# Moving the weight buffers of a two-layer kernel to other addresses in SBUF

## The chip, the cores and the metric

The kernel runs on one core of a Trainium2 chip. The metric is the device time of one execution in microseconds; three runs of the kernel before gave 1261.37, 1260.05 and 1260.09 us, median 1260.09 us. One of these executions was taken with the profiler.

## The reference

The reference computes two layers of a transformer on a sequence of 512 tokens, model width 1024, all in float32. Layer 0 has sparse attention (16 heads of 64, an indexer that keeps the best 128 keys of each query, a T5 bias); layer 1 has latent attention (16 heads, queries and keys of 96, values of 64). Each is followed by a feed-forward block with a causal convolution of width 3. Cut to what matters here:

```
for layer in range(2):
    h = rms_norm(x, norm_mix[layer])
    m = mixer_a(h, ...) if layer == 0 else mixer_b(h, ...)   # both end in  out @ w_out
    x = x + m
    h = rms_norm(x, norm_ffn[layer])
    u = h @ f_w_up[layer]                                    # 1024 -> 5632
    u = conv_b + sum(conv_w[j] * shifted(u, j) for j in range(3))
    gate, val = split(u, 2)
    x = x + (silu(gate) * val) @ f_w_down[layer]             # 2816 -> 1024
```

The feed-forward width is 2816, that is 22 tiles of 128.

## The kernel before

Every large product is done in three matmuls, so that the result is close to float32: each operand x is split into a rounded part x_hi and the rest x_lo, and `product3` (its three matmuls are lines 1715, 1716 and 1717) adds hi*hi, then s_hi*m_lo, then s_lo*m_hi into the same bank of PSUM. The first operand after the destination is the stationary one (loaded into the array, PEld in the profile), the second is streamed past it.

Weights come in units of up to 1 MB (128 partitions of 2048 words). The unit with number u goes to slot u % 2 of three buffers, each `[128, 2, SLOT]` words with SLOT = 2048:

- SyncE starts the DMA into `raw[:, s]` (`load`, line 389) once the unit two before it has been split;
- ScalarE copies it, rounded, to `w_hi[:, s]` (`hi`, line 571);
- VectorE writes `w_lo = raw - w_hi` (`lo`, line 937). Ten units of the first stage are split by GpSimd instead (line 527).

TensorE waits for `w_lo_done` before it uses a slot. Everything is ordered by semaphores written by hand; each engine has its own list of instructions, in program order.

The stages, in order of time: input products of mixer A (to about 190 us; here the tokens `h_hi`, `h_lo` are stationary and the weights are streamed in stretches of 512 columns); attention A (to about 270); its output product; feed-forward 0, up (325 to 566; weights stationary, `h_hi`, `h_lo` streamed) and down (567 to 675; weights stationary, `a_hi`, `a_lo` streamed); the latent stages of mixer B (688 to 775; its first product streams the weights in stretches of 416 columns), attention B, its output product, and feed-forward 1. At the joins between stages VectorE adds the result to `xT` (line 1139) and prepares `h_lo` (line 943) for each of eight tiles, while ScalarE prepares `h_hi` (line 579) and GpSimd sums squares held in `v` (line 501).

All tensors in SBUF are laid one behind another in the order in which the code declares them, each starting at the next multiple of 32 bytes; a nested `with ExitStack() as scope` gives its space back at its end, so that what is declared behind it lies over it (`act` over `ckv_hi` and others; `probs` and `toep` over `h_hi` and `h_lo`; `a_hi` and what follows over `qT`). Tensors named `pad_...` are never written or read. In the built program `xT` starts 16,512 bytes into each partition. Counted from there, the places of the operands modulo 512 bytes are 0 for `raw`, `w_hi`, `w_lo`, `act`, `h_hi`, `h_lo`, `probs`, `toep_a1`, `toep_b0`, `toep_b1`, `a_hi` and `a_lo`, and 64 for `v`, `rope_tmp` and `cv`. Modulo 2048 bytes, `raw`, `w_hi`, `w_lo` and `act` are at 0, `h_hi`, `h_lo`, `probs`, `a_hi` and `a_lo` at 512, `v` at 64.

Of the kernel before, what the change touches and what calls it, by code (L numbers as in the profile page):

```python
# [21 lines left out]
F32 = mybir.dt.float32  # L22
F32R = mybir.dt.float32r
BF16 = mybir.dt.bfloat16
ALU = mybir.AluOpType
# [3 lines left out]
P = 128  # L29
S = 512  # L30
# [26 lines left out]
B_DOWN = Q_LORA + KV_LORA + ROT  # L57
# [5 lines left out]
CT = 2 * FT  # L63
UP_STEPS = FT // 2
SLOT = 2048

BLOCK_N = [128 * (b + 1) for b in range(T)]
ROW = sum(BLOCK_N)
# [24 lines left out]
U_UP = [U_AOUT + KD, 0]  # L93
# [22 lines left out]
def unit_words(u):  # L116
# [5 lines left out]
    if u < U_DOWN[0]:  # L122
        return SLOT
    if u < U_B:
# [3 lines left out]
    if u < U_UP[1]:  # L128
        return D
    return SLOT if u < U_DOWN[1] else D  # L130

# [32 lines left out]
def hybrid_layers_kernel(nc, xt, vectors, t5_bias, a_in_wide, a_in_small, a_w_out, b_w_down, b_w_uq,  # L164
# [4 lines left out]
    with ExitStack() as ctx:  # L169
        def sb(name, shape, dt=F32, scope=ctx):  # L170
            return scope.enter_context(nc.sbuf_tensor(name, shape, dt))

        def sem(name):
            return ctx.enter_context(nc.semaphore(name))


        xT = sb("xT", [P, KD, S])
        raw = sb("raw", [P, 2, SLOT])
        w_hi = sb("w_hi", [P, 2, SLOT], F32R)
        w_lo = sb("w_lo", [P, 2, SLOT], F32R)  # L180

        with ExitStack() as scope:
            sb("pad_act", [P, 5, S], F32, scope)
# [36 lines left out]
        sq = v[:].rearrange("p t (a n) -> p (t a) n", n=S)  # L220

        rope_tmp = sb("rope_tmp", [P, 2, H * HALF])
        sb("pad_level", [P, 112])


        with ExitStack() as scope:
# [17 lines left out]

        with ExitStack() as scope:
            qT = sb("qT", [P, 16, S], F32, scope)
        a_hi = sb("a_hi", [P, 2, S], F32R)
        a_lo = sb("a_lo", [P, 2, S], F32R)
        u_in = sb("u_in", [P, 4, S + 4])
        cv = sb("cv", [P, 4, S])  # L250
        rbc = sb("rbc", [P, S])
        diag = sb("diag", [P, T, P])
        sb("pad_q", [P, 16 * S - (4 * S + 4 * (S + 4) + 4 * S + 2 * S)])
        ps = ctx.enter_context(nc.psum_tensor("ps", [P, 8, 512], F32))


# [24 lines left out]
        w_raw = [sem("w_raw0"), sem("w_raw1")]  # L281
# [100 lines left out]
        @block.sync  # L382
        def _(sp):
            def load(u, src, dst=None, k=None):

                s = u % 2 if k is None else k
                if not isinstance(u, int) or u >= 2:
                    sp.wait_ge(w_lo_done, u - 1)
                sp.dma_start(dst if dst is not None else raw[:, s, :], src).then_inc(w_raw[s], 16)

            sp.dma_start(gain, vectors[:, 0:G_COLS]).then_inc(v_in, 16)
            sp.dma_start(xT[:, 0:2, :], xt[:, 0:2, :]).then_inc(x_in[0], 16)
            for s in range(2):
                load(U_A + s, a_in_small[s], raw[:, s, 0:4 * A_SMALL])
            sp.dma_start(bucket, bucket_of).then_inc(b_in, 16)
            sp.dma_start(t5, t5_bias).then_inc(b_in, 16)
            for j in range(1, 4):
                sp.dma_start(xT[:, 2 * j:2 * j + 2, :], xt[:, 2 * j:2 * j + 2, :]).then_inc(x_in[j], 16)
            sp.wait_ge(w_lo_done, U_A + 1)
            sp.dma_start(raw[:, 0, 0:D], a_in_wide[0, 0, :, 0:D]).then_inc(w_first, 16)  # L400
            sp.dma_start(raw[:, 0, D:SLOT], a_in_wide[0, 0, :, D:SLOT]).then_inc(w_raw[0], 16)
            sp.dma_start(vec[:, G_COLS:V_COLS], vectors[:, G_COLS:V_COLS]).then_inc(c_in, 16)
            sp.dma_start(con[:], constants).then_inc(c_in, 16)
            load(U_A + 3, a_in_wide[0, 1])
            for c in range(2, len(A_CHUNKS)):
                for s in range(2):
                    load(U_A + 2 * c + s, a_in_wide[c - 1, s])
                if c == 2:

                    sp.wait_ge(rows_sb, 2)  # L410
                    sp.dma_start(bias_rows, bias_sb).then_inc(bias_out, 16)
                if c == 3:
                    sp.wait_ge(bias_out, 16)
                    sp.dma_start(bias_tiles, bass.AP(bias_rows.tensor, P - 1, [[640, H], [-1, P], [1, S]]))\
                      .then_inc(bias_out, 16)
            for k in range(2):
                load(U_AOUT + k, a_out_v[k], raw[:, k, 0:D])

            def load_toep(i, e):
                sp.dma_start(toep[i % 2][e][:, :], bias_tiles[2 * i + e]).then_inc(toep_in[i % 2][e], 16)  # L420

            sp.wait_ge(bias_out, 32)
            sp.wait_ge(pa_half, len(A_CHUNKS))
            load_toep(0, 0)
            load_toep(0, 1)
            load_toep(1, 0)
            sp.wait_ge(pa_done, 4 * (len(A_CHUNKS) - 1))
            load_toep(1, 1)
            for i in range(2, PAIRS):
                for e in range(2):  # L430

                    sp.wait_ge(l_ok[0], 6 * (i - 2) + 5 + e)
                    load_toep(i, e)
            for k in range(2, KD):
                load(U_AOUT + k, a_out_v[k], raw[:, k % 2, 0:D])

            def load_ffn(l):
                with sp.Fori(0, UP_STEPS) as i:
                    for s in range(2):
                        load(U_UP[l] + 2 * i + s, f_up[l, i, s], raw[:, s, :], s)  # L440
                with sp.Fori(0, FT // 2) as i:
                    for s in range(2):
                        load(U_DOWN[l] + 2 * i + s, down_v[l][2 * i + s], raw[:, s, 0:D], s)

            load_ffn(0)

            load(U_B, b_w_down[0].rearrange("p (a n) -> p a n", a=2),
                 raw[:, 0, :].rearrange("p (a n) -> p a n", a=2)[:, :, 0:2 * B_DOWN])
            load(U_B + 1, b_w_down[1], raw[:, 1, 0:4 * B_DOWN])
            for s in range(2):  # L450
                load(U_B + 2 + s, b_uq_v[s], raw[:, s, 0:QW])
            for s in range(2):
                load(U_B + 4 + s, b_w_ukv[0, :, s * D:(s + 1) * D], raw[:, s, 0:D])
            for k in range(KD):
                load(U_BOUT + k, b_out_v[k], raw[:, k % 2, 0:D])
            load_ffn(1)

            for k in range(KD):
                sp.wait_ge(x_new[4], k + 1)
                sp.dma_start(out[:, k, :], xT[:, k, :]).then_inc(out_sem, 16)  # L460
            sp.wait_ge(out_sem, 16 * KD)
# [3 lines left out]
        def _(pool):  # L465
# [57 lines left out]
            for u in range(POOL_LO[0], POOL_LO[1]):  # L523
                pool.wait_ge(w_hi_done, u + 1)
                pool.wait_ge(w_lo_done, u)
                s = u % 2
                pool.tensor_tensor(w_lo[:, s, :], raw[:, s, :], w_hi[:, s, :].bitcast(F32), ALU.subtract)\
                    .then_inc(w_lo_done, 1)
            for u in range(UNITS):
                normed(0, u)  # L530
# [1253 lines left out]
```

## Time and profile before

| what | value |
|---|---|
| median of three runs | 1260.09 us |
| the profiled execution | 1261.37 us, of it 1259.6 us span |
| TensorE (PE) busy | 1220.7 us, 97% of the span |
| VectorE, ScalarE, GpSimd busy | 767.4, 547.5, 212.6 us |
| TensorE's granted clock, mean | 0.996 of 2.4 GHz |
| moved by DMA | 110.83 MB, 88 GB/s |

The span runs from the first to the last instruction of the profiled execution; what lies around it is 1261.37 - 1259.6 = 1.8 us. Matmuls overlap, and their ends are modelled: the time that one adds is the distance between the starts of two neighbours, not the duration shown for it. A group of the profile is a line of the code with the tile written and the tiles read; the order of the names in `h_hi,w_hi` does not tell which is stationary, the code does.

### The profile page before, as it was taken

The numbers are of one execution on the slowest core, as the hardware profiler recorded it, in microseconds if no ns is written. First come the engines' busy times: TensorE is split into PE (matmuls) and PEld (weight loads), VectorE is DVE, ScalarE is ACT, GpSimd is POOL, SyncE is SP. The second block draws the span as 40 slices with busy tenths as digits, with TensorE's granted clock in tenths as the row PEclk, the third lists the DMA queues.
The fourth block names the chain that finished last, engine by engine and source line by source line (L and its number), as shares of the span: only waits on it lengthen the run. The fifth ranks groups of instructions, "written<-read, shape, count | busy, mean of one in ns | idle before, by whom it ended". The sixth has DMA issues, their size and how long they took to land.

```text
span 1259.6 us, 17234 instructions
## 1 busy us (share of the span) xinstructions
PE 1220.7 (97%) x6072; PEld 980.3 (78%) x6080; DVE 767.4 (61%) x1337; ACT 547.5 (43%) x933; POOL 212.6 (17%) x262
## 2 busy tenths in 40 slices
PE   6999999999999999999999878999999999999998
PEld 4868886678788888888888766768788888887887
DVE  3577895754766666563337678762775666664334
ACT  5554435653633333332325676652543333343232
POOL 4314243430400000000003572430400000000000
PEclk9999999999999999999999999999999999999999
DMA  6432212204222232213332110012322222222323
GB/s 232 155 98 87 96 68 68 73 29 134 100 100 100 76 107 84 100 50 100 100 100 97 59 35 1 1 35 90 113 99 100 100 100 100 74 75 84 100 89 111
DMA packets 25120, 110.83 MB, mean 88 GB/s; under 512 B 2752, under 2 KB 3136, under 8 KB 17776
## 3 DMA queue, kind: packets, MB, share of 16 engines
q1 hardware_dynamic: 25072, 110.21, 25.8%
q8 instruction: 28, 0.46, 0.1%
q14 instruction: 20, 0.16, 0.0%
HBM read 108.06 MB, written 6.33 MB: 91 GB/s over the span
## 4 chain that ended last, share of the span: by engine, by line
PE 86%; DVE 6%; POOL 2%; ACT 2%; issue 2%; DMA 1%; SPq 0%; DVEq 0%; ACTq 0%; POOLq 0%
PE ps L1715 24%; PE ps L1717 24%; PE ps L1716 24%; PE ps L1476 3%; PE ps L1495 3%; PE ps L1376 2%; PE ps L1364 2%; DVE h_lo L943 1%; DVE xT L1139 1%; PE ps L1459 1%; DVE w_lo L937 1%; PE ps L1449 1%; PE ps L1359 1%; DMA xT<-in_xt 1%; POOL rope_tmp L479 1%
## 5 line engine op out<-in xcount | busy, mean ns | idle before, releaser
L937 DVE TENSOR_TENSOR w_lo<-raw,w_hi 128x1024 fp32r<-128x1024 f32 (+4 forms) x114 | 194.7, 1708 | 255.1 <-ACT w_hi L571 255.1
L1715 PE MATMUL ps<-h_hi,w_hi 128*128 128x512 f32 (+1 forms) x712 | 278.4, 391 | 2.4 <-DVE w_lo L937 2.4
L1716 PE MATMUL ps<-h_lo,w_hi 128*128 128x512 f32 (+1 forms) x712 | 277.7, 390 | 0.0
L571 ACT ACTIVATE w_hi<-raw 128x1024 fp32r<-128x1024 f32 (+4 forms) x124 | 177.7, 1433 | 229.8 <-PE ps L1717 229.5
L1717 PE MATMUL ps<-h_hi,w_lo 128*128 128x512 f32 (+1 forms) x712 | 277.5, 390 | 0.0
L1715 PE MATMUL ps<-a_hi,w_hi 128*128 128x512 f32 x480 | 188.0, 392 | 2.1 <-DVE w_lo L937 1.5
L1716 PE MATMUL ps<-a_lo,w_hi 128*128 128x512 f32 x480 | 186.8, 389 | 0.0
L1717 PE MATMUL ps<-a_hi,w_lo 128*128 128x512 f32 x480 | 186.8, 389 | 0.0
L1715 PEld LDWEIGHTS ps<-h_hi,w_hi 128*128 128x128 f32 (+1 forms) x712 | 133.5, 188 | 31.8 <-DVE w_lo L937 3.2
L1717 PEld LDWEIGHTS ps<-h_hi,w_lo 128*128 128x128 f32 (+1 forms) x712 | 133.6, 188 | 28.6 <-issue 0.6
L1716 PEld LDWEIGHTS ps<-h_lo,w_hi 128*128 128x128 f32 (+1 forms) x712 | 133.6, 188 | 28.1 <-issue 0.4
L786 ACT ACTIVATE cv<-u_in,vec 128x512 f32<-128x512 f32 x88 | 71.5, 816 | 187.4 <-DVE u_in L1165 185.4
L501 POOL TENSOR_TENSOR v<-v 128x512 f32<-128x512 f32 x28 | 50.7, 1810 | 462.5 <-ACT v L583 442.6
L1165 DVE TENSOR_TENSOR u_in<-ps,rbc 128x512 f32<-128x512 f32 x88 | 60.2, 688 | 94.3 <-PE ps L1717 91.5
L1715 PEld LDWEIGHTS ps<-a_hi,w_hi 128*128 128x128 f32 x480 | 90.1, 188 | 23.8 <-DVE w_lo L937 2.4
L1717 PEld LDWEIGHTS ps<-a_hi,w_lo 128*128 128x128 f32 x480 | 90.1, 188 | 18.8
L1716 PEld LDWEIGHTS ps<-a_lo,w_hi 128*128 128x128 f32 x480 | 90.1, 188 | 18.3
L1715 PE MATMUL ps<-w_hi,h_hi 128*128 128x512 f32 (+1 forms) x256 | 102.0, 398 | 2.4 <-DVE w_lo L937 1.9
L1717 PE MATMUL ps<-w_hi,h_lo 128*128 128x512 f32 (+1 forms) x256 | 99.5, 389 | 0.0
L1716 PE MATMUL ps<-w_lo,h_hi 128*128 128x512 f32 (+1 forms) x256 | 99.0, 387 | 0.0
L520 POOL TENSOR_SCALAR probs<-probs,inv_sum 128x256 f32<-128x256 f32 (+3 forms) x128 | 66.8, 538 | 106.7 <-DVE inv_sum L1024 106.5
L664 ACT ACTIVATE probs<-probs,neg_max 128x256 f32<-128x256 f32 (+3 forms) x128 | 70.5, 553 | 18.6 <-DVE neg_max L1014 18.4
(189 smaller groups left out, 1525.3 us busy)
## 6 DMA issues: line engine op xcount, KB each, us to landing
raw<-in_f_up SPq DMA_DIRECT2D x44, 1024.0 KB, 4.8
raw<-in_f_w_down SPq DMA_DIRECT2D x44, 512.0 KB, 3.4
raw<-in_a_in_wide SPq DMA_DIRECT2D x13, 1024.0 KB, 4.9
bias_tiles<-bias_rows SPq DMA_DIRECT2D x1, 4096.0 KB, 20.1
raw<-in_a_w_out SPq DMA_DIRECT2D x8, 512.0 KB, 3.4
raw<-in_b_w_out SPq DMA_DIRECT2D x8, 512.0 KB, 3.4
xT<-in_xt SPq DMA_DIRECT2D x4, 512.0 KB, 6.3
toep_b<-bias_tiles SPq DMA_DIRECT2D x8, 256.0 KB, 2.8
```

Of the source, the lines that this page charges most:

```text
L501: pool.tensor_tensor(total, total, sq[:, ORDER[n][k], :], ALU.add).then_inc(sq_sum, 1)
L520: ins = pool.tensor_scalar(x, x, inv_sum[:, slot, e, p:p + 1], 1.0, ALU.mult, ALU.mult)
L571: sc.activation(w_hi[:, s, 0:n], raw[:, s, 0:n], ACT.Copy).then_inc(w_hi_done, 1)
L664: ins = sc.activation(x, x, ACT.Exp, bias=neg_max[:, slot, e, p:p + 1], scale=-1.0, accum_out=sums[:, slot, e, p:p + 1])
L786: sc.activation(cv[:, q, :], u_in[:, q, 2:2 + S], ACT.Identity, bias=conv[:, 3, bass.ds(ch, 1)], scale=conv[:, 2, bass.ds(ch, 1)])\
L937: dve.tensor_tensor(w_lo[:, s, 0:n], raw[:, s, 0:n], w_hi[:, s, 0:n].bitcast(F32), ALU.subtract)\
L1165: dve.tensor_tensor(u_in[:, q, 2:2 + S], ps[:, 4 + q, :], rbc[:], ALU.mult).then_inc(f_in[l], 1)
L1476: ins = pe.transpose(ps[:, turn_bank(u, e), c * P:(c + 1) * P], probs[slot][:, e, c * P:(c + 1) * P], ident)
L1495: ins = pe.matmul(ps[e * DH:(e + 1) * DH, 7, b * P:(b + 1) * P], v[:, kb, h * DH:(h + 1) * DH], probsT[u % 2][:, e, c * P:(c + 1) * P], st ...
L1715: pe.matmul(dst, s_hi, m_hi, start=start, stop=False)
L1716: pe.matmul(dst, s_hi, m_lo, start=False, stop=False)
L1717: return pe.matmul(dst, s_lo, m_hi, start=False, stop=stop)
```

## The change

Each slot of `raw`, `w_hi` and `w_lo` becomes 16 words (64 bytes) longer, so slot 1 starts 64 bytes later within its buffer, and 96 words of padding follow each of the three buffers. `pad_level` (112 words ahead of `h_hi`) goes away, and `pad_a` (112 words ahead of `a_hi`, behind the place where `qT` begins) comes in; `pad_q` is shortened by the same 112 words. The remaining edits name the 2048 words that are used, `0:SLOT`, where the whole slot was named before.

```diff
+SLOT_PITCH = SLOT + 16
...
-        raw = sb("raw", [P, 2, SLOT])
-        w_hi = sb("w_hi", [P, 2, SLOT], F32R)
-        w_lo = sb("w_lo", [P, 2, SLOT], F32R)
+        raw = sb("raw", [P, 2, SLOT_PITCH])
+        sb("pad_raw", [P, 96])
+        w_hi = sb("w_hi", [P, 2, SLOT_PITCH], F32R)
+        sb("pad_w_hi", [P, 96])
+        w_lo = sb("w_lo", [P, 2, SLOT_PITCH], F32R)
+        sb("pad_w_lo", [P, 96])
...
         rope_tmp = sb("rope_tmp", [P, 2, H * HALF])
-        sb("pad_level", [P, 112])
...
             qT = sb("qT", [P, 16, S], F32, scope)
+        sb("pad_a", [P, 112])
         a_hi = sb("a_hi", [P, 2, S], F32R)
...
-        sb("pad_q", [P, 16 * S - (4 * S + 4 * (S + 4) + 4 * S + 2 * S)])
+        sb("pad_q", [P, 16 * S - (112 + 4 * S + 4 * (S + 4) + 4 * S + 2 * S)])
...
-                sp.dma_start(dst if dst is not None else raw[:, s, :], src).then_inc(w_raw[s], 16)
+                sp.dma_start(dst if dst is not None else raw[:, s, 0:SLOT], src).then_inc(w_raw[s], 16)
...
-                        load(U_UP[l] + 2 * i + s, f_up[l, i, s], raw[:, s, :], s)
+                        load(U_UP[l] + 2 * i + s, f_up[l, i, s], raw[:, s, 0:SLOT], s)
...
-                 raw[:, 0, :].rearrange("p (a n) -> p a n", a=2)[:, :, 0:2 * B_DOWN])
+                 raw[:, 0, 0:SLOT].rearrange("p (a n) -> p a n", a=2)[:, :, 0:2 * B_DOWN])
...
-                pool.tensor_tensor(w_lo[:, s, :], raw[:, s, :], w_hi[:, s, :].bitcast(F32), ALU.subtract)\
+                pool.tensor_tensor(w_lo[:, s, 0:SLOT], raw[:, s, 0:SLOT], w_hi[:, s, 0:SLOT].bitcast(F32), ALU.subtract)\
```

The places that result, in bytes from the start of `xT`, modulo 2048, with the shift of each:

| tensor | before | after | shift |
|---|---|---|---|
| raw, slot 0 / 1 | 0 / 0 | 0 / 64 | 0 / 64 |
| w_hi, slot 0 / 1 | 0 / 0 | 512 / 576 | 512 / 576 |
| w_lo, slot 0 / 1 | 0 / 0 | 1024 / 1088 | 1024 / 1088 |
| act | 0 | 1536 | 1536 |
| v, rope_tmp | 64 | 1600 | 1536 |
| h_hi, h_lo, probs, toep_a1, toep_b0, toep_b1, qT | 512 | 1600 | 1088 |
| a_hi, a_lo, u_in | 512 | 0 | 1536 |

On each of the five engines the program has the same instructions in the same order as before.

## Rows read from the trace of the kernel before

**Rows 1.** The page, busy time and share of the span of each engine.

```profile
PE 1220.7 (97%) x6072; PEld 980.3 (78%) x6080; DVE 767.4 (61%) x1337; ACT 547.5 (43%) x933; POOL 212.6 (17%) x262
```

**Rows 2.** The page, the chain that ended last, by engine.

```profile
PE 86%; DVE 6%; POOL 2%; ACT 2%; issue 2%; DMA 1%; SPq 0%; DVEq 0%; ACTq 0%; POOLq 0%
```

**Rows 3.** PE busy and its granted clock, in stretches of feed-forward and input products.

```profile
340.00:560.00 220.00, 220.00 (x973) 1.00 0.26 92
570.00:665.00 95.00, 95.00 (x421) 1.00 0.31 99
```

**Rows 4.** Groups by line and shape: xcount, busy us, mean ns, idle before.

```profile
L1715 PE MATMUL ps<-h_hi,w_hi 128*128 128x512 f32 x704 | 274.5, 390 | 2.4 <-DVE w_lo L937 2.4
L1715 PE MATMUL ps<-a_hi,w_hi 128*128 128x512 f32 x480 | 188.0, 392 | 2.1 <-DVE w_lo L937 1.5 <-DVE a_lo L1106 0.6
L1715 PE MATMUL ps<-w_hi,h_hi 128*128 128x512 f32 x224 | 89.9, 401 | 0.5 <-DVE w_lo L964 0.5
...
L937 DVE TENSOR_TENSOR w_lo<-raw,w_hi 128x2048 fp32r<-128x2048 f32 x45 | 105.4, 2342 | 58.0 <-ACT w_hi L571 58.0
L937 DVE TENSOR_TENSOR w_lo<-raw,w_hi 128x1024 fp32r<-128x1024 f32 x63 | 79.8, 1267 | 193.6 <-ACT w_hi L571 193.6
```

**Rows 5.** Timeline of PE in feed-forward 0, up: start, duration, operation.

```profile
450.26 0.39 PE L1715 MATMUL ps<-h_hi,w_hi 128*128 128x512 f32 x1
...
451.62 0.39 PE L1715 MATMUL ps<-h_hi,w_hi 128*128 128x512 f32 x1
```

**Rows 6.** The same in the input products of mixer A.

```profile
109.76 0.39 PE L1715 MATMUL ps<-w_hi,h_hi 128*128 128x512 f32 x1
...
112.48 0.39 PE L1715 MATMUL ps<-w_hi,h_hi 128*128 128x512 f32 x1
```

**Rows 7.** The same in the 416-column products of mixer B.

```profile
694.68 0.35 PE L1715 MATMUL ps<-w_hi,h_hi 128*128 128x416 f32 x1
...
695.24 0.35 PE L1715 MATMUL ps<-w_hi,h_hi 128*128 128x416 f32 x1
...
695.81 0.35 PE L1715 MATMUL ps<-w_hi,h_hi 128*128 128x416 f32 x1
...
696.37 0.35 PE L1715 MATMUL ps<-w_hi,h_hi 128*128 128x416 f32 x1
```

**Rows 8.** Line 1715, weight loads: ns min/median/max.

```profile
L1715 PEld LDWEIGHTS ps<-h_hi,w_hi x712: 140/188/238, 9.9 to 1134.6; 128*128 128x128 f32 x176, 128*72 128x72 f32 x2
L1715 PEld LDWEIGHTS ps<-a_hi,w_hi x480: 186/188/188, 270.3 to 1255.4; 128*128 128x128 f32 x160
```

**Rows 9.** DMA issues: size, median us to landing.

```profile
raw<-in_f_up SPq DMA_DIRECT2D x44, 1024.0 KB, 4.8
raw<-in_f_w_down SPq DMA_DIRECT2D x44, 512.0 KB, 3.4
...
toep_b<-bias_tiles SPq DMA_DIRECT2D x8, 256.0 KB, 2.8
...
rope_tmp<-bias_tiles SPq DMA_DIRECT2D x4, 256.0 KB, 2.7
toep_a<-bias_tiles SPq DMA_DIRECT2D x4, 256.0 KB, 2.9
```

**Rows 10.** Timeline, the splitting of one down unit, its load, its next use.

```profile
601.55 1.23 DVE L937 TENSOR_TENSOR w_lo<-raw,w_hi 128x1024 fp32r<-128x1024 f32 x1 [3.55 <-ACT w_hi L571]
...
602.95 0.33 SPq L389 DMA_DIRECT2D raw<-in_f_w_down  x1
...
611.34 1.06 ACT L571 ACTIVATE w_hi<-raw 128x1024 fp32r<-128x1024 f32 x1 [3.80 <-PE ps L1717]
```

**Rows 11.** Timeline of DVE and POOL at the join before feed-forward 0.

```profile
316.35 0.75 DVE L943 SCALAR_TENSOR_TENSOR h_lo<-xT,vec,h_hi 128x512 fp32r<-128x512 f32 x1
317.01 0.68 DVE L1139 TENSOR_TENSOR xT<-xT,ps 128x512 f32<-128x512 f32 x1
317.61 1.19 DVE L943 SCALAR_TENSOR_TENSOR h_lo<-xT,vec,h_hi 128x512 fp32r<-128x512 f32 x1
318.72 0.67 DVE L1139 TENSOR_TENSOR xT<-xT,ps 128x512 f32<-128x512 f32 x1
...
316.54 10.76 POOL L501 TENSOR_TENSOR v<-v 128x512 f32<-128x512 f32 x6 [46.22 <-ACT v L583]
```

**Rows 12.** The chain of waits at that join: start, us, what.

```profile
316.44 0.66 DVE h_lo L943
...
317.70 1.10 DVE h_lo L943
...
319.40 1.10 DVE h_lo L943
...
321.10 1.11 DVE h_lo L943
322.21 2.25 DVE w_lo L937
```

## Prediction

> **What bounds the kernel now.** I read the page first: TensorE is busy 1220.7 of 1259.6 us [rows 1], and the chain that ended last runs on it for 86%, on VectorE for 6%, GpSimd and ScalarE 2% each, DMA 1% [rows 2]. Then stretches within stages: in feed-forward up and down TensorE is busy all the time at a granted clock of 1.00, the 2.4 GHz level [rows 3]. The groups by shape give the size of it: 512-column matmuls come 3 x 704, 3 x 480 and 3 x 224 times (lines 1715, 1716 and 1717 alike), 4224 in all [rows 4]. What one adds is the distance of starts: six of them from 450.26 to 451.62 us make 0.2267 us each [rows 5], twelve from 109.76 to 112.48 also 0.2267 [rows 6]. So 4224 x 0.2267 = 957.6 us, 76% of the span, is a steady beat, and what the change does to that beat decides; the other engines matter at the joins between stages alone.
>
> **The change part by part.** It removes, adds and moves no instruction; each reads and writes as many words as before, and each DMA moves as many bytes in as many rows. Only places in SBUF differ. The question is therefore for each engine: does any row show that its time depends on the place?
>
> TensorE. In the two feed-forward blocks (3 x 704 up, 3 x 352 of the 3 x 480 down) and the output products (3 x 128) the weights are stationary: half of the loads then start at slot 1, 64 bytes past the 512-byte grid on which all of them lie now. The streamed `h_hi` and `h_lo` move to 64 past the grid as well, `a_hi` and `a_lo` stay on it. In the input products the roles are swapped. Three observations:
> - The beat is 0.2267 us with weights stationary and tokens streamed (places 0 and 512 modulo 2048) and also with the roles swapped [rows 5, 6]. There is no difference by which place does what.
> - The 416-column products of mixer B stream weights from starts 1664 bytes apart, so 0, 128, 256 and 384 bytes off the grid in turn. Each group of three takes 0.56 to 0.57 us (694.68, 695.24, 695.81, 696.37) whatever its start [rows 7]. That is 0.188 us a matmul, the duration of a weight load.
> - A weight load takes 188 ns in a beat of 226.7 [rows 8]. The 38.7 ns between are cover: a load from the new place could grow by a fifth and cost nothing.
> I take 0 for TensorE. No 512-column product has an operand at exactly 64 past the grid, so both bounds stay open. Above: the longest load of this kind of weights took 238 ns [rows 8]; if each from slot 1 did, (238 - 226.7) x 1776 = +20 us (1776 is half of the 3552 matmuls with stationary weights). Below: 512 columns at 2.4 GHz are 213.3 ns, so the beat has 13.3 ns that are not columns; if they were a conflict of places and went, 13.3 x 4224 = -56 us. I take the value of rows 5 to 7 as the nearest, since they vary the place and show nothing.
>
> The page "TensorE: Matmul & The Clock Gate" of the Trainium skill (section "Back-to-back issue gap") gives an isolated matmul N / 2.4 + 2.5 ns, that is 215.8 for 512 columns, and knows no term for where operands lie. The trace shows 226.7, so there are 10.9 ns which that formula does not explain; were they due to places, 4224 of them would be worth 46 us. By the formula itself the change gives nothing.
>
> VectorE, ScalarE, GpSimd on the weights. `w_lo` of 2048 words takes 2342 ns in the mean, of 1024 words 1267 [rows 4]: 1024 more words for 1075 ns, 1.05 ns a word, with both sources and the destination at the same place modulo 2048. A conflict that cost a second pass would show as twice that. I see no room for a gain, and take 0. They are hidden besides: in the feed-forward stretches TensorE never stopped for them [rows 3]. If each `w_lo` took a tenth less, the joins would gain about 0.2 us each, under 1 us in all.
>
> DMA. Every load for slot 1 now lands 64 bytes past the grid. The trace has this very case: `rope_tmp` lies 64 past it, `toep_a1` and the `toep_b` on it; the same 256 KB land in 2.7 us against 2.9 and 2.8 [rows 9]. So 0. The cover, should it be wrong: a down unit is free at 601.55 + 1.23 = 602.78, its load starts at 602.95, lands 3.4 later at 606.35, and ScalarE takes it at 611.34 after waiting for TensorE [rows 10]. The spare time is 5.0 us; a load would have to take 2.5 times as long before anything waited. The loads queue behind no other instruction of SyncE that has moved.
>
> The page "DMA: Bandwidth & Descriptors" of the Trainium skill ("How a descriptor splits into AXI transactions") speaks against the change: a row that does not start on a multiple of 256 bytes costs beats for the bytes before its start. The built program has `raw` at 32,896 bytes, which is 128 past such a multiple already; slot 1 goes to 192 past it. By the page that is 2 more beats of 32 bytes on some 260, an estimate of 0.04 us on 4.8, and it would be hidden. No row here can resolve that.
>
> GpSimd beside VectorE at the joins. While GpSimd sums squares (from 316.54), `h_lo` takes 1.19 us instead of 0.75, yet the addition to `xT` keeps its 0.67 to 0.68 [rows 11]. On the chain the four late pieces cost 1.10, 1.10, 1.11 and 2.25 us, where undisturbed ones are 0.66 and 1.23 (of a 1024-word `w_lo`, rows 10) [rows 12]. That is 0.44 x 3 + 1.02 = 2.3 us at this join; with three joins of this form, 7.0 us. It hits instructions with two sources in SBUF, at two quite different pairs of places (`xT`/`h_hi`, `raw`/`w_hi`), and spares the one whose other source is PSUM: so the ports are shared, not the places, and new places change nothing. The page "SBUF — State Buffer" of the Trainium skill ("Who interferes with whom") says the same, that a VectorE instruction with two SBUF inputs contends with a GpSimd instruction that reads SBUF. A rule of banks instead would let this go to zero.
>
> The sum: 0 + 0 + 0 + 0 on the profiled execution, 1259.6 of span and 1.8 around it, 1261.4 us. The median of the runs is 1.3 lower, so I forecast 1260.1.
>
> **The rivals.**
> A, slower: the loads of weights from slot 1 outgrow their cover. The place is the feed-forward and the output products, the price the +20 us above, so 1280 us. It decides from (2.5 / 1776 =) 1.4 ns a matmul on, that is from a load of about 228 ns, 40 more than now. For it: no weight load in the trace starts there, and single loads of 238 ns exist. Against: the cover, and rows 7. The same answer holds if the streamed `h_hi` costs a few cycles from its new start: at 2.4 ns for 2112 matmuls 5 us, 1265.
> B, faster: the slowdown beside GpSimd is a conflict of places, and the new spread ends it: 1260.1 - 7.0 = 1253 us. Against it speaks that two unlike pairs suffer alike [rows 11, 12].
> C, faster: part of the 13.3 ns in the beat is such a conflict, as weights and `h` share the 512-byte grid now. All of it gives 1204 us; 0.6 ns a matmul would be enough to see. Against: the beat does not care which roles the places have [rows 5, 6].
> D: the DMA into slot 1 is slower, but hidden: no change in time, only rows 9 would differ. It lies within my forecast.
> E: the change does not do what it says. The built program does have the new places, so there is nothing left of this one.
>
> **How the numbers follow.** No change 0.84 (of it 0.02 on either side for a small shift that is more than the bound), A with its small form 0.09, B 0.04, C 0.03. A measurement of this kernel tells about 0.2%, 2.5 us, from no change: the three runs are within 1.3 us. That makes faster 0.04 + 0.03 + 0.02 = 0.09, slower 0.09 + 0.02 = 0.11, and 0.80 for the same. The likeliest case alone ranges from 1257.6 to 1262.6. For 8 in 10 I give 1257.3 to 1263.0, a little wider upwards, where A's small form begins; the far ends of A (1280) and C (1204) and B are left out with less than 2 in 10.
>
> **What would show it.** Right: distances of starts of 0.2267 us in the same three stages; weight loads at 188 ns with both slots; `w_lo` at about 1227 and 2290 ns where undisturbed; loads of 4.8 and 3.4 us; the same four long pieces at the join. Wrong: for A, weight loads above 226 ns in every other unit, or a longer beat where `h_hi` streams; for B, 0.75 us for `h_lo` beside a busy GpSimd; for C, a beat below 0.226. The forecast fails as a whole if any place in SBUF sets TensorE's beat, by as little as 1 ns a matmul.

## The result: 0.6% slower, through TensorE's beat

The changed kernel took 1269.91 us (median of 7 runs, 1268.12 to 1272.72). The kernel before, run again beside it, took 1263.65 us (median of 7, 1260.05 to 1265.38). The ratio is 1.0057, with a 95% interval of 1.0039 to 1.0077. I had forecast 1260.1 us and no change; the time lies above the range of 1257.3 to 1263.0.

The page of the changed kernel, its shares by engine, and under them the chain that ended last:

```profile
span 1268.6 us, 17242 instructions
PE 1230.6 (97%) x6080; PEld 980.8 (77%) x6080; DVE 767.5 (60%) x1337; ACT 547.5 (43%) x933; POOL 212.5 (17%) x262
PE 87%; DVE 6%; POOL 2%; issue 2%; ACT 2%; DMA 1%; SPq 0%; DVEq 0%; ACTq 0%; POOLq 0%
```

Against [rows 1], PE is busy 9.9 us longer and the span is 9.0 us longer. VectorE, ScalarE, GpSimd and the weight loads are busy as long as before to within 0.5 us. So the added time is in the matmuls of TensorE. The groups by line and shape (count, busy us, mean ns of one, idle before; lines are four higher than before):

```profile
L1720 PE MATMUL ps<-h_lo,w_hi 128*128 128x512 f32 x704 | 275.6, 391 | 0.0
L1719 PE MATMUL ps<-h_hi,w_hi 128*128 128x512 f32 x704 | 275.4, 391 | 2.0 <-DVE w_lo L941 2.0
L1719 PE MATMUL ps<-a_hi,w_hi 128*128 128x512 f32 x480 | 189.5, 395 | 1.9 <-DVE w_lo L941 1.5 <-DVE a_lo L1110 0.4
L1719 PEld LDWEIGHTS ps<-a_hi,w_hi 128*128 128x128 f32 x480 | 90.2, 188 | 25.2 <-DVE w_lo L941 2.4 <-DVE a_lo L1110 1.3 <-issue 1.0
L941 DVE TENSOR_TENSOR w_lo<-raw,w_hi 128x2048 fp32r<-128x2048 f32 x45 | 105.4, 2341 | 58.0 <-ACT w_hi L575 58.0
L1719 PE MATMUL ps<-w_hi,h_hi 128*128 128x512 f32 x224 | 90.4, 404 | 0.0
L941 DVE TENSOR_TENSOR w_lo<-raw,w_hi 128x1024 fp32r<-128x1024 f32 x63 | 79.8, 1267 | 198.5 <-ACT w_hi L575 198.5
```

Against [rows 4] the means of the matmuls rise by 1 to 3 ns, while `w_lo` keeps 1267 ns and 2341 for 2342. The weight load keeps its 188 ns [rows 8]. The modelled durations hide the size of it; the starts give it. Feed-forward 0, up, in the changed kernel: first a stretch with the weights in slot 0, then one in slot 1 (start, duration):

```profile
345.41 0.39 PE L1719 MATMUL ps<-h_hi,w_hi 128*128 128x512 f32 x1
...
353.65 0.39 PE L1719 MATMUL ps<-h_hi,w_hi 128*128 128x512 f32 x1
...
357.08 0.39 PE L1719 MATMUL ps<-h_hi,w_hi 128*128 128x512 f32 x1
...
365.24 0.39 PE L1719 MATMUL ps<-h_hi,w_hi 128*128 128x512 f32 x1
```

Both pairs are 36 matmuls apart: 8.24 us, or 228.9 ns each, in slot 0, and 8.16 us, or 226.7 ns, in slot 1. Slot 0 is the slow one here, and it is slot 1 that the change moved off the grid. In down it is the other way round (slot 0, then slot 1):

```profile
576.15 0.39 PE L1719 MATMUL ps<-a_hi,w_hi 128*128 128x512 f32 x1
...
577.53 0.39 PE L1719 MATMUL ps<-a_hi,w_hi 128*128 128x512 f32 x1
...
580.93 0.39 PE L1719 MATMUL ps<-a_hi,w_hi 128*128 128x512 f32 x1
581.61 0.40 PE L1719 MATMUL ps<-a_hi,w_hi 128*128 128x512 f32 x1
...
584.41 0.40 PE L1719 MATMUL ps<-a_hi,w_hi 128*128 128x512 f32 x1
...
586.51 0.39 PE L1719 MATMUL ps<-a_hi,w_hi 128*128 128x512 f32 x1
```

In slot 1, 21 matmuls take 4.90 us, 233.3 ns each. In slot 0, which begins at 576.15, 15 take 3.40 us, 226.7 ns; its first six take 1.38 us, 230.0 ns each, so the slow beat of the slot 1 before runs on into them. What the two stages have in common is the distance between the two operands. In up, slot 0 holds weights on the grid while `h` is streamed from 64 bytes past it, and in slot 1 both are 64 past it. In down, `a` is on the grid and so is slot 0, while slot 1 is 64 past it.

The other engines and the DMA do not set this beat. The slot 1 stretch above, in two halves (busy time of PE, PEld, DVE, ACT, POOL, then granted clock, DMA share, GB/s):

```profile
581.60:584.40 2.80, 2.80 (x13) 2.26 (x12) 1.50 (x2) 1.58 (x2) 0.00 (x0) 1.00 0.07 28
584.40:587.20 2.80, 2.80 (x13) 2.26 (x12) 0.33 (x1) 0.00 (x0) 0.00 (x0) 1.00 0.61 186
```

VectorE and ScalarE work in the first half and hardly in the second, DMA the other way round, GpSimd in neither. The beat is 233.3 ns in both: 12 matmuls take 2.80 us up to 584.41, 9 take 2.10 us after it.

Where the 9.0 us went, as the distance from the start of the first to the start of the last 512-column matmul of each stage, both kernels by the profile:

(The first products with `w_out`, which run between pieces of attention, are left out of the output products.)

| stage | before, us | after, us |
|---|---|---|
| input products of mixer A | 185.77 | 187.40 |
| output products A, B | 38.61, 38.62 | 39.14, 39.18 |
| up 0, 1 | 243.17, 243.16 | 244.09, 244.09 |
| down 0, 1 | 120.58, 120.57 | 122.55, 122.55 |
| from down 0 to output product B | 171.56 | 172.18 |

That is 1.6 + 1.1 + 1.9 + 3.9 + 0.6 = 9.1 us; the rest of the kernel differs by 0.1 in all. Down alone holds 3.9 of it, with a quarter of the 512-column matmuls.

The rest came out as forecast. The DMA loads (KB each, median us to landing):

```profile
raw<-in_f_up SPq DMA_DIRECT2D x44, 1024.0 KB, 4.8
raw<-in_f_w_down SPq DMA_DIRECT2D x44, 512.0 KB, 3.4
```

are those of [rows 9], and at the join before feed-forward 0 the pieces beside a busy GpSimd are those of [rows 11, 12]:

```profile
318.24 0.74 DVE L947 SCALAR_TENSOR_TENSOR h_lo<-xT,vec,h_hi 128x512 fp32r<-128x512 f32 x1
318.90 0.68 DVE L1143 TENSOR_TENSOR xT<-xT,ps 128x512 f32<-128x512 f32 x1
319.50 1.19 DVE L947 SCALAR_TENSOR_TENSOR h_lo<-xT,vec,h_hi 128x512 fp32r<-128x512 f32 x1
...
324.05 2.32 DVE L941 TENSOR_TENSOR w_lo<-raw,w_hi 128x1024 fp32r<-128x1024 f32 x1
```

### The profile page after: what moved, and what is told of

It reads as the page before. It is cut to its first block, busy times and chain, and to the rows that moved or that the text cites. A ratio compares the mean times of both kernels' runs of the same rounds, so it can differ in the third digit from the quotient of the medians.

```text
span 1268.6 us, 17242 instructions
## 1 busy us (share of the span) xinstructions
PE 1230.6 (97%) x6080; PEld 980.8 (77%) x6080; DVE 767.5 (60%) x1337; ACT 547.5 (43%) x933; POOL 212.5 (17%) x262
## 4 chain that ended last, share of the span: by engine, by line
PE 87%; DVE 6%; POOL 2%; issue 2%; ACT 2%; DMA 1%; SPq 0%; DVEq 0%; ACTq 0%; POOLq 0%
PE ps L1719 25%; PE ps L1720 24%; PE ps L1721 24%; PE ps L1480 3%; PE ps L1499 3%; PE ps L1380 2%; PE ps L1368 2%; DVE h_lo L947 1%; DVE xT L1143 1%; PE ps L1463 1%; DVE w_lo L941 1%; PE ps L1363 1%; PE ps L1453 1%; PE ps L1691 1%; POOL rope_tmp L483 1%
```

## The experiments

Below, a distance is the place of the streamed operand minus that of the stationary one, in bytes. Theory R says that this distance sets the beat. A beat is an average of starts over a steady stretch of the stage.

### The change taken apart

**u1_no_pitch**, the change without the longer slots:

```diff
-SLOT_PITCH = SLOT + 16
+SLOT_PITCH = SLOT
-        sb("pad_raw", [P, 96])      (and the same for w_hi, w_lo)
+        sb("pad_raw", [P, 128])
```

> The change without its 16 words a slot: both slots of each weight buffer lie on the 512-byte grid, h_hi and h_lo stay 64 bytes past it, a_hi and a_lo on it. Theory R (TensorE's beat depends on how far the streamed operand lies from the stationary one: 0 gives 226.7 ns a matmul, +64 bytes 229.0, -64 bytes 233.4): feed-forward up 229.0 in both slots, down 226.7 in both, input products 233 in both; together 2112 x 2.3 + 672 x 6 = about +9 us over before, ratio 1.007. Rival S (what costs is the place of slot 1 itself): every stage back at 226.7, ratio 1.000. Rival M (what costs is the spread of the buffers over 2048 bytes): as the whole change, 1.006, with the same slots slow as there.

Measured: 1269.09 us against 1262.67, ratio 1.0045 (1.0028 to 1.0062). Up and down, 36 matmuls each:

```profile
370.75 0.39 PE L1719 MATMUL ps<-h_hi,w_hi 128*128 128x512 f32 x1
...
378.99 0.39 PE L1719 MATMUL ps<-h_hi,w_hi 128*128 128x512 f32 x1
...
581.83 0.39 PE L1719 MATMUL ps<-a_hi,w_hi 128*128 128x512 f32 x1
...
589.99 0.39 PE L1719 MATMUL ps<-a_hi,w_hi 128*128 128x512 f32 x1
```

8.24 us, 228.9 ns, in up; 8.16 us, 226.7 ns, in down. Up was at 228.9 in both slots, the input products at 233.3. All beats are those of theory R. The expected ratio of 1.007 lies above the interval: the sum over all matmuls was too high. It comes out high in the change too, where 528 matmuls of up at 2.3 ns are 1.2 us a layer and the stage grew by 0.9. Where the rest goes was not followed. Rival S falls: with no slot off the grid, up is slower than in the change. Rival M falls: the slow slots are others.

**u2_pitch_only**, the longer slots, with `h` back on the grid:

```diff
+        sb("pad_level", [P, 112])
-        sb("pad_a", [P, 112])
```

> The 16 words a slot and the pads of 96 words, with h_hi, h_lo, a_hi and a_lo on the 512-byte grid as before. Theory R: slot 0 at 226.7 ns in all stages; slot 1, which lies at 64, at 233.4 where it is stationary (up, down, output products) and 229 where it is streamed (input products): 1056 x 6.7 + 720 x 6.7 + 336 x 2.3 = about +12.7 us, ratio 1.010, slower than the change itself. Rival S: slot 1 slow in all stages, by what the change shows in down, also about 1.010, but the input products too at 233. Rival M: as the whole change, 1.006.

Measured: 1274.14 us, ratio 1.0088 (1.0071 to 1.0104), slower than the change itself. Up in slot 0, then in slot 1:

```profile
367.77 0.39 PE L1719 MATMUL ps<-h_hi,w_hi 128*128 128x512 f32 x1
...
375.96 0.39 PE L1719 MATMUL ps<-h_hi,w_hi 128*128 128x512 f32 x1
...
378.68 0.40 PE L1719 MATMUL ps<-h_hi,w_hi 128*128 128x512 f32 x1
...
387.07 0.40 PE L1719 MATMUL ps<-h_hi,w_hi 128*128 128x512 f32 x1
```

Slot 1 takes 8.39 us, 233.1 ns. Slot 0 takes 8.19 us for the same number, since its first matmuls still keep the slow beat. The input products were at 229.1 in slot 1, not at 233 as rival S would have it, because the roles are swapped there.

**u3_spread_only**, the spread of the buffers over 2048 bytes alone:

```diff
-SLOT_PITCH = SLOT + 16
+SLOT_PITCH = SLOT
-        sb("pad_raw", [P, 96])      (and the same for w_hi, w_lo)
+        sb("pad_raw", [P, 128])
+        sb("pad_level", [P, 112])
-        sb("pad_a", [P, 112])
```

> Only the spread over 2048 bytes: slots of 2048 words, 128 words of padding behind each buffer, pad_level as before, so that all large operands lie on the 512-byte grid. Theory R, if a distance counts only modulo 512 bytes or less: 226.7 ns everywhere, ratio 1.000. Rival M: up to 1.006.

Measured: 1263.31 us, ratio 1.0004 (0.9992 to 1.0015), 226.67 ns in up and down. The spread costs and brings nothing.

### Which distances cost

Each of the six versions in this part was run once, so they are read by their beats, not by their times.

From here on the kernel before is the base; only the two numbers in these lines differ, and `pad_q` is shortened to match:

```diff
-        sb("pad_level", [P, 112])
+        sb("pad_level", [P, 96])     # h_hi, h_lo 64 bytes ahead of the grid
...
+        sb("pad_a", [P, 32])         # a_hi, a_lo 64 bytes past it
```

**s1_minus64**, those numbers.

> The kernel before with h_hi and h_lo 64 bytes ahead of the grid and a_hi and a_lo 64 bytes past it. Theory R: the signs turn round: up (streamed minus stationary -64) 233.4 ns in both slots, down and output products (+64) 229.0 in both, input products (h stationary, +64) 229: +14 + 3 + 2 = about +19 us, some 1280 to 1284 us. Rival N (only the size of the distance counts, not its sign): up 229, down and input products 233, about +19 us as well, told apart by the beats.

Measured once: 1278.02 us. Up, then down, 36 matmuls each:

```profile
366.65 0.39 PE L1717 MATMUL ps<-h_hi,w_hi 128*128 128x512 f32 x1
...
375.05 0.39 PE L1717 MATMUL ps<-h_hi,w_hi 128*128 128x512 f32 x1
...
580.93 0.39 PE L1717 MATMUL ps<-a_hi,w_hi 128*128 128x512 f32 x1
...
589.17 0.39 PE L1717 MATMUL ps<-a_hi,w_hi 128*128 128x512 f32 x1
```

8.40 us, 233.3 ns, and 8.24 us, 228.9 ns. The sign counts, as theory R said; rival N falls.

**t32**: `pad_level` 120, `pad_a` 112 words.

> The kernel before with h_hi and h_lo 32 bytes past the grid and a_hi and a_lo 32 bytes ahead of it. Distances (streamed minus stationary): up +32, input products -32, down -32. If the cost grows with the distance: half of what 64 bytes cost, up near 227.8, down and input products near 230. If a line of 64 bytes or more is what counts, 226.7 at +32 or at -32, or at both.

Measured: 1284.85 us, the slowest of all. 36 matmuls of up, then of down:

```profile
370.67 0.39 PE L1717 MATMUL ps<-h_hi,w_hi 128*128 128x512 f32 x1
...
379.07 0.39 PE L1717 MATMUL ps<-h_hi,w_hi 128*128 128x512 f32 x1
...
583.65 0.40 PE L1717 MATMUL ps<-a_hi,w_hi 128*128 128x512 f32 x1
...
592.05 0.40 PE L1717 MATMUL ps<-a_hi,w_hi 128*128 128x512 f32 x1
```

8.40 us both times, 233.3 ns at +32 as at -32. The input products were at 233.2. A smaller distance is not cheaper: the cost does not grow with it. All 4224 matmuls at 6.6 ns more would be 28 us; the time is 22 us above the 1262.97 of the kernel before.

**t128**: `pad_level` 144, `pad_a` 64 words.

> The kernel before with h_hi and h_lo 128 bytes past the grid and a_hi and a_lo 128 ahead of it: up +128, input products -128, down -128. If the places repeat every 128 bytes, 226.7 ns everywhere and the time of before; if only every 512 bytes, other beats than 226.7, perhaps longer than 233.

Measured: 1283.0 us. Up was at 233.3 ns in the first layer and 232.4 in the second, down at 232.4 in both, the input products at 232.7; 12 matmuls taken alone give 231.7 to 233.3. So places do not repeat every 128 bytes.

**t96**: `pad_level` 136, `pad_a` 40 words.

> The kernel before with h_hi and h_lo 96 bytes past the grid and a_hi and a_lo 256 bytes past it: up +96, input products -96, down +256. If places repeat every 128 bytes, up takes what down takes in the run with -32, the input products what up takes there with +32, and down 226.7. If they repeat only every 512 bytes, down shows it.

Measured: 1278.86 us. 36 matmuls of up at +96, then of down at +256:

```profile
370.97 0.39 PE L1717 MATMUL ps<-h_hi,w_hi 128*128 128x512 f32 x1
...
379.37 0.39 PE L1717 MATMUL ps<-h_hi,w_hi 128*128 128x512 f32 x1
...
585.18 0.39 PE L1717 MATMUL ps<-a_hi,w_hi 128*128 128x512 f32 x1
...
593.34 0.39 PE L1717 MATMUL ps<-a_hi,w_hi 128*128 128x512 f32 x1
```

233.3 ns at +96, 226.7 at +256: a distance of 256 bytes costs nothing.

**t192**: `pad_level` 160, `pad_a` 32 words.

> h_hi and h_lo 192 bytes past the grid, a_hi and a_lo 320 past it: up +192, input products -192, down +320. If places repeat every 256 bytes, up behaves as -64 (233.3 ns), input products and down as +64 (229.0): about +19 us, as the run with -64 and +64. If not, other beats.

Measured: 1277.7 us, up at 233.3, down at 229.0, the input products at 229.1. That is the run with -64 and +64 again: places repeat every 256 bytes.

**t16w**: both weight buffers shifted inside their tensors, `a` by 32 bytes.

```diff
-        w_hi = sb("w_hi", [P, 2, SLOT_PITCH], F32R)
+        w_hi = sb("w_hi", [P, 2 * SLOT + 128], F32R)[:, 4:4 + 2 * SLOT].rearrange("p (s n) -> p s n", s=2)
```

> w_hi and w_lo 16 bytes past the grid in both slots, h on it, a 32 past it: up -16, down +16, input products +16. If a distance of 16 bytes counts as 32 did: 233 ns in all, about +27 us. If pieces smaller than 32 bytes do not count: 226.7, the time of before. A beat below 226.7 would show that the kernel before is not at the best place.

Measured: 1276.23 us. Up (-16) was at 233.3 ns. Down (+16) was at 226.67 in layer 0 and 228.3 in layer 1, the input products (+16) at 231.7. My expectation of 233 at both signs was wrong for +16, which costs less, and not the same in both layers. No beat went below 226.67.

### Whose distance it is

**x_lo64**, with `w_lo`, `h_lo` and `a_lo` alone 64 bytes past the grid (further pads, left out here, put what follows back on it):

```diff
+        sb("pad_w_hi", [P, 16])
         w_lo = sb("w_lo", [P, 2, SLOT_PITCH], F32R)
+            sb("pad_hl", [P, 16], F32, scope)
             h_lo = sb("h_lo", [P, KD, S], F32R, scope)
+        sb("pad_al", [P, 16])
         a_lo = sb("a_lo", [P, 2, S], F32R)
```

> The kernel before with the lower parts alone (w_lo, h_lo, a_lo) 64 bytes past the grid, the upper parts on it. Each group of three matmuls then is (stationary hi, streamed hi), (stationary hi, streamed lo), (stationary lo, streamed hi), with distances of the own pair of 0, +64 and -64. If the distance that counts is that of a matmul's own two operands, the three take 226.7, 229 or more and 233: a mean near 229.7 in all stages, 4224 x 3.0 = about +12 us, ratio 1.010. If it is that of the operand being streamed and the one that is loaded beside it for the next matmul, all distances are 0 (hi beside hi, lo beside lo, hi beside hi) and the beat stays 226.7 ns, ratio 1.000.

Measured: 1277.53 us, ratio 1.0104 (1.0083 to 1.0125). 36 matmuls of up:

```profile
369.74 0.40 PE L1722 MATMUL ps<-h_hi,w_hi 128*128 128x512 f32 x1
...
378.06 0.40 PE L1722 MATMUL ps<-h_hi,w_hi 128*128 128x512 f32 x1
```

8.32 us, 231.1 ns; down 231.2 and 232.3, the input products 231.3. So the distance to the operand that is loaded beside the stream for the next matmul is not what counts, or not alone: it is 0 throughout here. A matmul's own two operands fit the direction, but they would give 229.7, and 231.1 to 232.3 came. Here alone the places also change from one matmul to the next, and that may cost by itself; this was not taken apart. So whose distance it is stays open in part. In all other versions the upper and lower parts lie alike, and their readings do not hang on it.

### Ways out

**f256**, the change with slots that are 256 bytes longer in place of 64:

```diff
-SLOT_PITCH = SLOT + 16
+SLOT_PITCH = SLOT + 64
```

(without the pads of 96 words and `pad_a`, with `pad_level`.)

> The change made with 64 words a slot in place of 16, no pads behind the buffers and pad_level kept: the buffers lie where the change puts them, but slot 1 is 256 bytes past the 512-byte grid instead of 64, and h_hi, h_lo, a_hi, a_lo are on it. Theory R, places equal modulo 256 bytes cost nothing: 226.7 ns in every stage, ratio 1.000. If only equality modulo 512 counted, slot 1 would be slow: up to 233, ratio up to 1.009.

Measured: 1263.18 us against 1262.88, ratio 0.9999 (0.9990 to 1.0008). Up in slot 1:

```profile
379.84 0.39 PE L1716 MATMUL ps<-h_hi,w_hi 128*128 128x512 f32 x1
...
388.00 0.39 PE L1716 MATMUL ps<-h_hi,w_hi 128*128 128x512 f32 x1
```

8.16 us, 226.7 ns. Longer slots cost nothing as long as they are longer by a multiple of 256 bytes.

**c_align**, `con` and `v` put on the grid too:

```diff
+        sb("pad_con", [P, 120])
         con = sb("con", [P, C_COLS])
+        sb("pad_v", [P, 120])
         v = sb("v", [P, T, D])
-        sb("pad_level", [P, 112])
```

> The kernel before with con (the identity matrix of the transposes) and v on the 512-byte grid too, where they are 32 and 64 bytes off before. The attention stages take their transposes and value products from them. Theory R allows a gain there if the beat of these short matmuls is set by places; since 128 columns are shorter than their weight load, I expect none: ratio 1.000, at best 0.998.

Measured: ratio 1.0000 (0.9990 to 1.0010). The attention stages gain nothing. No version was found that beats the kernel before; with all large operands at the same place modulo 256 bytes it runs at the lowest beat seen.

The distances together, steady beats in ns of a 512-column matmul, modulo 256 bytes:

| distance | beat | seen in |
|---|---|---|
| 0 | 226.7 | before, after (up slot 1, down slot 0), u3_spread_only, f256 (slot 1), t96 (down) |
| +16 | 226.7 to 231.7 | t16w |
| +64 | 229.0 | after (up, slot 0), u1_no_pitch, s1_minus64, t192 |
| +32, -32, +96, -16, -64 | 233.3 | t32, t96, t16w, s1_minus64, t192, after (down) |
| 128 | 232.4 to 233.3 | t128 |
| -96 | 234.2 | t96 (input products) |

## Why the prediction was wrong

**The sum for TensorE failed**, all other terms held. The prediction put 0 for the places of its operands. The measured terms are +2.3 ns for matmuls of up in slot 0 (streamed operand 64 bytes past the stationary one) and +6.7 ns for those of down in slot 1 (64 bytes ahead of it); the input and output products have slow slots too. Up, down, input and output products hold 8.5 us of the 9.0.

**What it rested on was read too coarsely.** The prediction called the 416-column groups of [rows 7] indifferent: "0.56 to 0.57 us ... whatever its start". The two values alternate with the start. With the starts taken to the nanosecond, groups streamed from 0 or 256 bytes off the grid have a beat of 187.2 ns (median over the four token tiles) and those from 128 or 384 off have 190.3. The dependence on places was in the trace before, 3 ns large, in the one stage whose starts vary, and repeating every 256 bytes. I rounded it away and took the value for that of a weight load. In s1_minus64 and t192, where `h` lies 64 ahead of the grid or 192 past it, the two kinds change sides (191.0 and 187.0). These groups follow the distance too, with the same period, but by other values: for 416 columns +64 costs (191.0) and -64 does not (187.0), which is the reverse of 512 columns. Even with this row read rightly, neither the sign nor the size for 512 columns could have been taken from it, only that 0 was no safe term.

**The second support proved less than it seemed.** The beat was the same with the roles swapped [rows 5, 6]. But 0 and 512 modulo 2048 are the same place modulo 256, so both stages were at distance 0. The stages compared did not vary the cause.

**The bound above and the price of rival A rested on a wrong row.** The 238 ns that the prediction took for "the longest load of this kind of weights" [rows 8] belong to another shape, which the row mixes in. Line 1715's weight loads at the very start:

```profile
10.85 0.24 PEld L1715 LDWEIGHTS ps<-h_hi,w_hi 128*72 128x72 f32 x1 [0.19 <-issue]
...
13.34 0.14 PEld L1715 LDWEIGHTS ps<-h_hi,w_hi 128*72 128x72 f32 x1
```

They are 72 columns wide, and those that take 0.24 us all start before 13.3 us, where matmuls of 512 columns start 0.43 us apart. That is the pace which f256 shows at a granted clock of 0.50, the 1.2 GHz level (nine from 33.01 to 36.84 us). So 238 ns was a matter of the clock and says nothing of places.

**Rival A had the engine, not the mechanism.** Its main form, weight loads from slot 1 that outgrow their cover, did not happen: they stayed at 188 ns, and in up it is slot 0 that is slow. That slot 1 is slow in down, as this form had it, is luck. Its small form (2.4 ns for 2112 matmuls as `h_hi` streams from its new start, 1265 us) names the same size as the 2.3 ns of up, for twice the matmuls that took it, and has no place for down, where the cost is three times as large. A got 0.09.

**Rival B** is refuted: `h_lo` beside GpSimd takes 1.19 us in both kernels. **Rival C**, that the beat would fall below 226.7, is refuted for all distances tried; its idea that two operands share a grid was right with the sign turned round, since sharing is what keeps the beat low. **D** did not even show: the loads land in 4.8 and 3.4 us.

**The forecast's level.** 1260.1 us was the median of three runs; the same kernel took 1263.65 us beside the change, itself above the range, and 1262.67 to 1262.97 in the later comparisons. So 3.6 us of the miss in time are not the change. The ratio is what the forecast has to answer for: 0.57%, with at least 0.39, against the 0.2% that it called no change.

## What to carry to other kernels

When TensorE sets the time, compare the places of its two operands modulo 256 bytes of a partition, for each slot of each buffer: where they are equal, the beat of these 512-column matmuls was 226.7 ns, elsewhere mostly 229 to 234, up to 3%. The distances were tried for 512 columns in float32; for 416 columns equal places were the fast ones too, but -64 was as fast. Padding a buffer is harmless in multiples of 256 bytes. A beat is to be read from starts over tens of matmuls, at the full resolution of the trace: 3 ns a matmul disappear in a column of hundredths of a microsecond, and are up to 12 us in a kernel with 4000 of them.

## What the runs showed of the hardware

- The beat depends on the distance of the operands with a period of 256 bytes and is not symmetric: +64 bytes gives 229.0 ns, -64 gives 233.3. In the changed kernel the load itself, 188 ns, and the granted clock of 1.00 (345 to 560 us and 570 to 670 us) are as before. Why these values stays open.
- The slow beat outlasts its cause: after slot 1 of down in the changed kernel, the first three to six matmuls at distance 0 were still slow (from 576.15, three starts apart by 230.7 ns in the mean; from 587.21, six by 231.5) before the beat fell to 226.7. From fast to slow there is no such delay (234.3 ns for the first three from 581.61).
- `t16w`, `t128` and `x_lo64` show different steady beats in the two layers at the same distances (226.7 and 228.3 in down; 233.3 and 232.4 in up; 231.2 and 232.3 in down), so something else than the distance takes part. It was not found.
- Kernels with equal beats differ by some us with the mean granted clock: the span was 1259.6 us for the kernel before at 0.996 and 1262.9 us for f256 at 0.992. Both have a beat of 226.7 ns in feed-forward; the difference is in how often the clock fell to 1.2 GHz outside it. Most of it lies in one place: from 31 to 37 us, in the input products, f256 ran 18 matmuls at a granted clock of 0.50, the kernel before 31 at 1.00. Just ahead, eight matmuls of one column were all that TensorE did from 28.3 to 32.0 us in f256 and from 28.8 to 31.7 in the kernel before; the clock fell in the first alone.
